# Two-stream encoder trunk on one core: the end of a differential-attention head reordered on TensorE, its output scaling on another engine

## The reference

```
q, k = rope(rmsnorm(q, g_q)) * 64**-0.5, rope(rmsnorm(k, g_k))     # per head two components of 64
s = einsum("bhcqd,bhckd->bhcqk", q, k);  p = softmax(s)
a = p[:, :, 0] - lam * p[:, :, 1]
o = a @ v                                                           # per head 128 columns
o = rmsnorm(o, g_sub) * (1 - lambda_init)
y = o.reshape(...) @ w_out
```

## Time and profile before

| what | value |
|---|---|
| time, median of 3 runs | 1863.31 us (1863.25 to 1863.38) |
| span of the profiled execution, first to last instruction | 1860.4 us |
| granted TensorE clock, mean | 1.000 |
| busy: PE, weight loads, DVE, ACT, POOL | 99%, 94%, 66%, 47%, 62% |
| attention heads in the span | from about 938 to 1320 us |
| instructions | 31456 |

### The profile page before, as it was taken

The page is one execution under the profiler, slowest core; times in us unless marked ns, Lnnn a source line. Parts: engine busy times, 40 slices in busy tenths (PEclk is TensorE's granted clock), DMA queues, the critical chain, the costliest instruction groups (busy, mean ns, idle before and its releaser), DMA issues.

```text
span 1860.4 us, 31456 instructions
## 1 busy us (share of the span) xinstructions
PE 1849.7 (99%) x10845; PEld 1742.0 (94%) x10845; DVE 1235.1 (66%) x2072; ACT 879.7 (47%) x1855; POOL 1162.6 (62%) x1533
## 2 busy tenths in 40 slices
PE   9999999999999999999999999999999999999999
PEld 8888889999999999999988888888889999999998
DVE  6756566768576757576876666666587575756663
ACT  6444343455444445454444444444465454444553
POOL 4453644468687878788843333333558788887885
PEclk9999999999999999999999999999999999999999
DMA  8789997549697977774475666664233535353534
GB/s 270 257 240 237 222 259 173 183 108 228 209 237 238 235 227 218 250 232 118 107 145 121 126 124 124 130 118 91 74 90 110 148 99 157 100 153 101 154 112 133
DMA packets 380153, 309.51 MB, mean 166 GB/s; under 512 B 14395, under 2 KB 322398, under 8 KB 379766
## 3 DMA queue, kind: packets, MB, share of 16 engines
q1 hardware_dynamic: 349472, 237.81, 42.1%
q0 software_dynamic: 28416, 69.21, 20.5%
q10 hardware_dynamic: 2134, 0.82, 0.2%
HBM read 302.16 MB, written 144.04 MB: 240 GB/s over the span
## 4 chain that ended last, share of the span: by engine, by line
PE 91%; DVE 5%; ACT 1%; issue 1%; DMA 1%; POOL 0%; SPq 0%; ACTq 0%; DVEq 0%; POOLq 0%
PE ps L974 51%; PE ps L884 26%; PE ps L1155 3%; PE ps L1312 3%; PE ps L1280 2%; PE ps L1302 1%; PE ps L1130 1%; PE ps L1214 1%; DVE rstd L1502 1%; PE ps L1164 1%; DVE sx L1554 0%; PE ps L1244 0%; DVE mx L2077 0%; DVE gt L1661 0%; DMA wk<-in_x_prompt_dram 0%
## 5 line engine op out<-in xcount | busy, mean ns | idle before, releaser
L974 PE MATMUL ps<-sx,wh 128*128 128x400 f32 (+1 forms) x2044 | 530.3, 340 | 0.9 <-POOL wl L808 0.5
L808 POOL TENSOR_TENSOR wl<-raw,wh 128x256 fp32r<-128x256 f32 (+1 forms) x432 | 355.6, 855 | 97.9 <-ACT wh L2243 96.4
L774 POOL CAST wh<-raw 128x256 fp32r<-128x256 f32 x248 | 102.5, 456 | 450.6 <-PE ps L884 424.9
L974 PEld LDWEIGHTS ps<-sx,wh 128*128 128x128 f32 x2044 | 373.4, 188 | 3.0 <-ACT gt_first L2258 0.9
L974 PE MATMUL ps<-sx,wl 128*128 128x400 f32 (+1 forms) x1022 | 347.6, 340 | 0.0
L808 POOL TENSOR_TENSOR wl<-raws,wh 128x256 fp32r<-128x256 f32 x328 | 283.8, 910 | 84.4 <-ACT wh L2243 84.0
L1715 DVE TENSOR_TENSOR h<-h,ps 128x400 f32<-128x400 f32 (+1 forms) x280 | 154.5, 559 | 131.5 <-PE ps L974 131.4
L974 PE MATMUL ps<-fx,wh 128*128 128x400 f32 (+1 forms) x904 | 235.3, 341 | 0.1
L884 PE MATMUL ps<-xh,wh 128*128 128x512 f32 (+1 forms) x752 | 211.2, 357 | 0.0
L884 PE MATMUL ps<-xl,wh 128*128 128x512 f32 (+1 forms) x752 | 207.3, 349 | 0.0
L778 POOL TENSOR_TENSOR wl<-raw,wh 128x256 fp32r<-128x256 f32 x248 | 198.8, 831 | 5.1
(11 more groups left out here) (330 smaller groups left out, 3552.0 us busy)
## 6 DMA issues: line engine op xcount, KB each, us to landing
in_sums<-in_ffn_w_in_dram SPq DMA_DIRECT2D x16, 1536.0 KB, 10.7
raw<-in_sums SPq DMA_DIRECT2D x96, 256.0 KB, 3.0
in_sums<-in_ffn_w_in_dram SPq DMA_DIRECT2D x16, 1280.0 KB, 7.2
raw<-in_ffn_w_in_dram SPq DMA_DIRECT2D x80, 256.0 KB, 3.0
raws<-in_sums SPq DMA_DIRECT2D x80, 256.0 KB, 3.1
raw<-out_sums SPq DMA_DIRECT2D x120, 128.0 KB, 2.6
raws<-in_ffn_w_in_dram SPq DMA_DIRECT2D x52, 256.0 KB, 3.1
raw<-in_m_w_in_dram SPq DMA_DIRECT2D x24, 512.0 KB, 4.8
```

What stands on the lines that cost most here:

```text
L774: ins = pool.tensor_copy(wh[:, slot, c], raw[:, slot, c])
L808: ins = pool.tensor_tensor(slot_of(n, 1)[:, c], raw_of(n)[:, c], slot_of(n, 0)[:, c].bitcast(F32), ALU.subtract)
L974: mm = pe.matmul(product_bank(layer, s, j), slot_of(n, low_w)[:, k * P:(k + 1) * P], x, start=(j in OPENS and k + q == 0), stop=(k == tile ...
```

## The change

On PE, the scores of the next head's tile 0 and part 0 of the output transposes move behind value tile 5 and `attend` 4; value tiles 6 and 7 follow them, and then part 1 of the output transposes, which before stood ahead of those two tiles. The last head keeps its order. The short transpose of the second sequence's tiles (i of 4 and 5) goes to bank 4 beside the full ones, and its wait for `o_ready` moves from `turn_attention` to `attend`. The reciprocal of the output roots moves on VectorE from `scale_output` into `invert_key_roots`, ahead of the reciprocal of the key roots. The scaling of the six outputs moves from VectorE to ScalarE, as six activations of the Copy kind with a scale per partition, behind `squared` 3; `turned` 4 now stands ahead of `squared` 3. The last head and the final outputs are scaled on VectorE as before.

```diff
             def turn_attention(hd, i, first):
-                if not (first and i == 0):
+                if i < 4 and not (first and i == 0):
                     pe.wait_ge(o_ready, hd * NQ + i)
                 pe.wait_ge(a_ready, hd * NQ + (i + 1))
                 for q, j in enumerate(OF_SEQ[Q_SEQ[i]]):
                     sz = TILES[j][2]
-                    dst = ps[:, 4, q * P:(q + 1) * P] if sz == P else ps[0:sz, 5, 0:P]
+                    dst = ps[0:sz, 4, q * P:(q + 1) * P] if q < 4 else ps[0:sz, 5, 0:P]
...
                 if i == 0:
                     pe.wait_ge(va_ready, hd * 3 + 3)
+                elif i > 3:
+                    pe.wait_ge(o_ready, hd * NQ + i)
...
                 turn_attention(hd, 4, first)
-                if not last:
-                    attn_scores(hd + 1, even, 0)
-                if not first:
+                if last:
                     turn_output(hd - 1, even, 0)
                 beside(values_block, 5, 6, (3, 0, 3))
                 attend(hd, odd, 4)
+                if not last:
+                    attn_scores(hd + 1, even, 0)
+                    if not first:
+                        turn_output(hd - 1, even, 0)
+                    values_block(6, 8)
                 if not first:
                     turn_output(hd - 1, even, 1)
-                beside(values_block, 6, 8, (3, 3, 6))
+                if last:
+                    beside(values_block, 6, 8, (3, 3, 6))
                 turn_attention(hd, 5, first)
...
-            def invert_key_roots(g, odd):
+            def invert_key_roots(g, odd, outputs=False):
                 ve.wait_ge(qk_root, g + 1)
+                if outputs:
+                    v(ve.reciprocal(rs[:, 0:NQ], rs[:, 0:NQ]))
+                    v.wait()
                 v(ve.reciprocal(qkr[:, odd, 2 * NQ:], qk2[:, 2 * NQ:]))
...
                 if not last:
-                    invert_key_roots(hd + 1, even)
+                    invert_key_roots(hd + 1, even, outputs=not first)
...
-                if not first:
+                if last:
                     scale_output(hd - 1, even)
-                if last:
                     add_tile(OUT1 + 2, EARLY[2], 3)
                 else:
                     maxima(hd + 1, even, 0)
...
+            def scale_output(hd, odd):
+                sc.wait_ge(lt_ready, hd + 3)
+                sc.wait_ge(o_ready, hd * NQ + NQ)
+                for i in range(NQ):
+                    ins = sc.activation(on(odd, i), on(odd, i), ACT.Copy, scale=rs[:, i:i + 1])
+                ins.then_inc(os_ready, 1)
...
-                sc.activation(at[0:META, i % 2, full, :], ps[0:META, 5, 0:P], ACT.Copy).then_inc(at_ready, 1)
+                short = ps[0:META, 5, 0:P] if full == 4 else ps[0:META, 4, full * P:(full + 1) * P]
+                sc.activation(at[0:META, i % 2, full, :], short, ACT.Copy).then_inc(at_ready, 1)
...
                 exps(hd, odd, 5)
+                turned(hd, 4)
                 squared(hd, odd, 3)
-                turned(hd, 4)
+                if not first and not last:
+                    scale_output(hd - 1, even)
                 if not first:
                     deliver(hd - 1, 0)
```

## The result

The changed kernel takes 1874.43 us (median of 5 runs), the kernel before 1863.25 in the same rounds: ratio 1.0058, 95% interval 1.0046 to 1.0070. The forecast was slower, by 5.4 us; the measured loss is 11.2 us, and 1874.43 lies above the range, which ended at 1871.6.

What follows compares the result with a forecast made beforehand. PE (TensorE), busy 99% of the span, was taken as the bound; +0.85 us a head (0.50 + 0.34 + 0.10 + 0.21 - 0.30), six heads +5.1, plus 0.3 for head 0, gave +5.4: 1868.7 us, range 1865.8 to 1871.6.

Steps and rivals of the forecast that it cites:

- (a): At part 1 of the output transposes: PE's wait for VectorE is removed, gaining 0.30 us a head.
- (b): Tile 5's transposes on PE newly wait for VectorE's `combine` 5, starting at S + 3.40; cost 0.50 us a head.
- (c): PE's next-head keys newly wait for VectorE's evacuation of the values, until S + 6.05; cost 0.34 us a head.
- S: Moment when PE is done issuing the next head's scores and part 0 of the output transposes starts; a clock's zero.
- (d): PE's second transposes of the values newly wait for ScalarE's first half, until S + 11.04; cost 0.10 us a head.
- Head 0: End of the first head, which delivers nothing and inverts no output roots: only a wait for `combine`, cost 0.3 us.
- (e): Output roots' reciprocal ahead of the keys' roots, in VectorE's gapless list: all on PE's path, cost 0.21 us a head.
- (f): Six output scalings moved to ScalarE: 1.3 to 1.9 us for six, hidden under PE's work, cost nothing.
- VectorE's idle time ahead of the maxima: Sign of being right: VectorE idle about 3.5 us before the maxima of the next head's scores.
- The wait at L884 for the evacuation: Sign of being right: PE waits at the next head's keys for VectorE's evacuation of the values (L1478).
- L1265 part 0 behind ScalarE: Sign of being wrong: PE's part 0 of the output transposes waits for ScalarE.
- ScalarE late with the scalings: Rival: scalings at 0.4 to 0.5 us each delay part 0 and all behind it; +7.8 us, 1871.1, chance 0.13.

## Why the prediction was right in its direction and wrong in its size

**(a)** held: the wait at part 1 went, 0.3 a head, and the run with that piece alone gained 2.1 us.

**(b)** held: 3.39 for 3.40, from the order of VectorE's list, as the run with `combine` 5 first shows.

**(c)** held in its end, 6.06 for 6.05 in the head shown and 6.17 in heads 1, 3 and 5. On the way there PE was up to 0.27 later than forecast at `attend` 5 (1087.57, S + 5.29, for 5.02), and so waited the less for the evacuation.

**(d)** failed, and carries most of the error. The step was: "ScalarE is done with the first half of the values at 1136.72 + 0.59 = 1137.31, 5.98 after the evacuation's start". It took the 5.98 us from the kernel before as a constant that could be shifted whole, and it counted VectorE's and ScalarE's instructions but not GpSimd's. Within these 5.98 us stood two VectorE steps that are free in the old order and blocked in the new one. Measured 11.96 for 11.04: 0.92 in each of heads 1 to 5, 4.6 us in all, and 0.1 in head 6; holding GpSimd alone took 0.8 of the 0.92 off. GpSimd's rows were in the trace of the kernel before, released by the very PE matmuls that the change moves, and no step of the forecast uses them. That wait was priced at "0.05 to 0.1" of doubt, so the range could not hold it.

**Head 0** failed too, by 0.5 us: 0.80 for the 0.3 forecast. Its term has the wait for `combine` 5 (0.2 measured) and puts at nothing the wait of the next head's scores of tile 1 for ScalarE's exponentials of tile 0, and what PE lost around it (0.6).

**(e)** held: 0.19 to 0.24 a head in the run that does only that. **(f)** held: hidden, 1.85 us for six, and the run with it undone differs by 1.5 us, which is (e) within the noise. Of the signs that were named, VectorE's idle time ahead of the maxima was 3.88 us for 3.5, and a head 50.15 for 49.2. The wait at L884 for the evacuation is named in no list of waits. In the head shown PE was 0.27 late at `attend` 5, so that under 0.1 of the 0.34 was left of it; in heads 1, 3 and 5 PE stood 0.4 us there, which the list puts down to issue. One sign of being wrong came up by its letter, L1265 part 0 behind ScalarE, in PE's weight loads. It says nothing here, since those loads wait as long behind VectorE in the kernel before.

So the direction was right by its mechanism, the new waits behind VectorE and ScalarE, and not by luck; the size was wrong, because one of these waits was 1.0 us long and not 0.1. Of the rivals none was the case: "ScalarE late with the scalings" gave 1871.1, near the range's end, but by a cause that the runs exclude. A further rival was missing, the one of an engine off the path whose start is tied to PE.

## What to carry to other kernels

When a step is moved, draw a clock for every engine and ask what each instruction's start is tied to; a chain may be shifted whole only against engines that are tied to the same event, and the one that is released by the moved engine slides underneath the others. Where an engine's list of matmuls between a producer and the first consumer of its chain shrinks from 5.0 to 2.9 us, as here, compare the chain's whole length (6 us here) with what is left before counting the wait that goes. A one-column VectorE step that took more than three times its usual time was the sign of the collision with GpSimd in this kernel, and moving GpSimd's start was a cheap mend once its new place was clear of such steps as well.

## What the runs showed of the hardware that was not expected

VectorE and GpSimd block each other, and only for some forms. Beside GpSimd's subtraction of two SBUF tensors (0.7 to 0.8 us each), VectorE steps with two inputs in SBUF took 0.79 for 0.22 (one column), 1.22 for 0.77 (528 columns), 0.75 for 0.16 (two columns) and 1.56 for 1.03 (two products); six scalings from SBUF to SBUF, with one tensor input, 2.33 for 1.27. The step of one column began at 1088.32 and ended at 1089.11, when the third of the four subtractions from 1086.98 on, 0.70 us each, was over (1089.09), which fits a wait for a whole instruction. The other way round, the four subtractions took 3.16 where they began inside the combine's last step, and 2.80 behind it. The maxima and the evacuation, which read PSUM, kept 1.24 and 0.98, and so did the reciprocal of two columns, 0.15. The Trainium skill (SBUF — State Buffer, Who interferes with whom) says that the two engines share one pair of ports as an exclusive lock, held for a whole instruction, which a VectorE operation takes in a two-port mode or with two inputs in SBUF; by that rule, the traces agree, including the steps that were not touched: the maxima read no operand from SBUF, the evacuation and the reciprocal one each.
